# Joining the two products of a weight tile's high part in the output projections of a 1,024-wide model kernel

## The reference

```python
return u @ w2 + b2                    # Conformer convolution
return o.reshape(...) @ w_o           # differential attention
return (y * g) @ w_o                  # RWKV-7 time mix
return (u * s) @ w_out                # spatial gating
...
x = x + g_m * rms_norm(y, norm_g[l, 1])     # first block
x = x + _rmsnorm(h, norm_gains[i, 1])       # second block
```

## Time and profile before

| | |
|---|---|
| median of 3 runs | 1,419.88 us (1,414.57 to 1,428.73) |
| profiled execution, span from the first to the last instruction | 1,420.2 us |
| busy: PE / DVE / ACT / POOL | 97% / 74% / 52% / 15% |
| granted TensorE clock, mean | 0.996 of full speed |
| Square of unit 0 to Square of unit 7: conv_down | 124.45 to 144.41 us |
| the same: att_out | 467.24 to 486.54 us |
| the same: rw_out | 907.82 to 926.13 us |
| the same: sgu_out | 1,203.07 to 1,220.00 us |

### The profile page before, as it was taken

How to read it: one execution, slowest core, us unless ns; L and a number is a source line. 1 busy time by engine, 2 the same in 40 slices (tenths; PEclk the granted TensorE clock), 3 DMA queues, 4 the chain that set the end, 5 groups by cost and what they waited for, 6 DMA issues and landing times.

```text
span 1420.2 us, 30753 instructions
## 1 busy us (share of the span) xinstructions
PE 1375.6 (97%) x11830; PEld 1310.7 (92%) x11830; DVE 1049.1 (74%) x1649; ACT 733.2 (52%) x1194; POOL 219.2 (15%) x232
## 2 busy tenths in 40 slices
PE   8999999999999999999999999999999999999997
PEld 6998899999988899999878888799999998999997
DVE  7988799987887889974787965777774556677743
ACT  4547555644556556664366442554444447544442
POOL 0000133310000223320000010113320000133300
PEclk9999999999999999999999999999999999999999
DMA  9874367797663547675322300346666433466661
GB/s 377 303 258 171 123 226 234 258 394 252 205 226 105 208 165 254 216 232 173 151 98 90 120 2 2 116 133 186 188 208 203 141 115 120 144 197 197 208 205 69
DMA packets 68434, 258.20 MB, mean 182 GB/s; under 512 B 7545, under 2 KB 9857, under 8 KB 67970
## 3 DMA queue, kind: packets, MB, share of 16 engines
q1 hardware_dynamic: 68354, 257.10, 54.2%
HBM read 256.01 MB, written 1.06 MB: 181 GB/s over the span
## 4 chain that ended last, share of the span: by engine, by line
PE 81%; DVE 11%; ACT 3%; issue 2%; DMA 2%; DVEq 0%; ACTq 0%
PE ps L740 21%; PE ps L742 20%; PE ps L741 20%; PE ps L757 3%; DVE lo L1919 2%; PE ps L701 2%; PE ps L703 1%; PE ps L702 1%; ACT hi L1370 1%; DMA modraw<-in_wmod 1%; DVE U L2508 1%; DMA modlast<-in_wmod 1%; DVE products L2506 1%; DVE modraw L1925 1%; PE ps L764 1%
## 5 line engine op out<-in xcount | busy, mean ns | idle before, releaser
L1919 DVE TENSOR_TENSOR lo<-raw,hi 128x1024 fp32r<-128x1024 f32 (+1 forms) x350 | 476.5, 1378 | 168.5 <-ACT hi L1370 167.8
L740 PE MATMUL ps<-OH,lo 128*128 128x256 f32 x1920 | 540.8, 282 | 6.2 <-DVE lo L1919 6.0
L742 PE MATMUL ps<-OH,hi 128*128 128x256 f32 x1920 | 534.8, 279 | 0.0
L741 PE MATMUL ps<-OL,hi 128*128 128x256 f32 x1920 | 534.8, 279 | 0.0
L1370 ACT ACTIVATE hi<-raw 128x1024 fp32r<-128x1024 f32 (+1 forms) x350 | 381.0, 1112 | 10.4 <-DMA raw<-in_w 6.1
L740 PEld LDWEIGHTS ps<-OH,lo 128*128 128x128 f32 x1920 | 362.0, 189 | 12.7 <-DVE lo L1919 9.9
L741 PEld LDWEIGHTS ps<-OL,hi 128*128 128x128 f32 x1920 | 362.4, 189 | 0.0
L742 PEld LDWEIGHTS ps<-OH,hi 128*128 128x128 f32 x1920 | 361.0, 188 | 0.0
L740 PE MATMUL ps<-GH,lo 128*128 128x256 f32 x704 | 196.3, 279 | 0.0
L742 PE MATMUL ps<-GH,hi 128*128 128x256 f32 x704 | 196.2, 279 | 0.0
L741 PE MATMUL ps<-GL,hi 128*128 128x256 f32 x704 | 196.2, 279 | 0.0
(11 more groups left out here) (389 smaller groups left out, 2059.5 us busy)
## 6 DMA issues: line engine op xcount, KB each, us to landing
raw<-in_w SPq DMA_DIRECT2D x288, 512.0 KB, 3.9
raw<-in_w SPq DMA_DIRECT2D x64, 704.0 KB, 5.3
modraw<-in_wmod SPq DMA_DIRECT2D x71, 512.0 KB, 5.2
modlate<-in_wmod SPq DMA_DIRECT2D x10, 512.0 KB, 4.0
modlast<-in_wmod SPq DMA_DIRECT2D x7, 512.0 KB, 4.5
modfirst_a<-in_wmod SPq DMA_DIRECT2D x4, 512.0 KB, 11.4
modfirst_b<-in_wmod SPq DMA_DIRECT2D x4, 512.0 KB, 12.1
l<-in_lora_in SPq DMA_DIRECT2D x1, 1536.0 KB, 6.2
```

Source lines behind the costliest of these rows:

```text
L740: pe.matmul(bank[:, 0:T], lo[:, r, w], oh[:, k0 + k], start=first, stop=False)
L741: pe.matmul(bank[:, 0:T], hi[:, r, w], ol[:, k0 + k], start=False, stop=False)
L742: ins = pe.matmul(bank[:, 0:T], hi[:, r, w], oh[:, k0 + k], start=False, stop=final)
L1919: dve.tensor_tensor(lo[:, s, 0:kt * P], raw[:, s, 0:kt * P], hi[:, s, 0:kt * P].bitcast(F32), ALU.subtract).then_inc(lo_made, 1)
```

## The change

In the four projections the products hi x OL and hi x OH become one product of 512 columns: `OH` and `OL` now are the halves of one tile `OB`, and the product writes a whole PSUM bank, the OH columns in its first half, the OL columns in its second. lo x OH goes on adding into the first half. So a chunk takes two products instead of three (256 chunks in all four projections). Then VectorE adds the two halves of the bank into one of two slots of `xt` (`add_halves`, one instruction a unit, 32 in all), and ScalarE squares and scales from `xt` and no longer from PSUM. `add_halves` stands in VectorE's step u behind the low part of the tile of u + 2, and ahead of the riding sums. It waits for the unit's products and for the evacuation of unit u - 2. ScalarE's evacuation waits for it. Two waits on `tt_made` become waits on a second count of `tm_made`; the order there is the same. All other layers keep their three products.

```diff
-        OH = at(2, "OH", [P, DC, T], F32R)
-        OL = at(2, "OL", [P, DC, T], F32R, plus=OPERAND)
+        OB = at(2, "OB", [P, 2, DC, T], F32R)
+        OH, OL = OB[:, 0], OB[:, 1]
...
+            def split_products(bank, r, w, oh, ol, k, first, final, wide):
+
+                if wide and first:
+                    pe.matmul(bank[:, :], hi[:, r, w], OB[:, :, k], start=True, stop=False)
+                    return pe.matmul(bank[:, 0:T], lo[:, r, w], oh[:, k], start=False, stop=final)
+                pe.matmul(bank[:, 0:T], lo[:, r, w], oh[:, k], start=first, stop=False)
+                if wide:
+                    return pe.matmul(bank[:, :], hi[:, r, w], OB[:, :, k], start=False, stop=final)
+                pe.matmul(bank[:, 0:T], hi[:, r, w], ol[:, k], start=False, stop=False)
+                return pe.matmul(bank[:, 0:T], hi[:, r, w], oh[:, k], start=False, stop=final)
...
                     c = 2 * i + r // 2 if down else 4 * i + r
-                    src = PS[r - 1 if down else r][:, 0:T]
+                    if not down:
+                        act.wait_ge(S("halves_added"), c + (DC * (n // 2) + 1))
+                    src = PS[r - 1][:, 0:T] if down else xt[:, 2 + r % 2]
...
+            def add_halves(i, r, u):
+
+                dve.wait_ge(mm_done, u + 1)
+                wait(dve, evac_done, u - 1)
+                dve.tensor_reduce(xt[:, 2 + r % 2], PS[r][:, :].rearrange("p (h t) -> p t h", h=2), AX_X, ALU.add
+                                  ).then_inc(S("halves_added"), 1)
+
             def rows_out(i, r, u):
+
+                add_halves(i, r, u)
...
-            layer("att_out", peel_all=True, made=1)
+            layer("att_out", add_halves, peel_all=True, made=1)
...
-            layer("rw_out", third=True)
+            layer("rw_out", add_halves, third=True)
...
-            layer("sgu_out", third=True, made=1)
+            layer("sgu_out", add_halves, third=True, made=1)
```

More of the change, by code:

```diff
@@ L686, in filter_waves, with two_units @@
                 pe.wait_ge(S("dft_hi"), DC + 1)
-            def two_units(name, oh, ol, fresh, after_chunk, beside):
+            def split_products(bank, r, w, oh, ol, k, first, final, wide):
[7 more added lines that the diff above has]
+                return pe.matmul(bank[:, 0:T], hi[:, r, w], oh[:, k], start=False, stop=final)
+            def two_units(name, oh, ol, fresh, after_chunk, beside, wide):
                 start = START[name]
@@ L700, in two_units @@
                     for r in range(2):
-                        pe.matmul(PS[r][:, 0:T], lo[:, r, w], oh[:, k], start=(k == 0), stop=False)
-                        pe.matmul(PS[r][:, 0:T], hi[:, r, w], ol[:, k], start=False, stop=False)
-                        ins = pe.matmul(PS[r][:, 0:T], hi[:, r, w], oh[:, k], start=False, stop=(k == KT - 1))
+                        ins = split_products(PS[r], r, w, oh, ol, k, k == 0, k == KT - 1, wide)
                         if k == KT - 1:
@@ L711, in layer @@
             def layer(name, oh, ol, between=None, peel_first=False, fresh=False, after_chunk=None, beside=0, amid=None,
-                      peel_all=False, together=False):
+                      peel_all=False, together=False, wide=False):
                 kt, start = TILES[name], START[name]
@@ L720, in body @@
                     if both:
-                        two_units(name, oh, ol, fresh, after_chunk, beside)
+                        two_units(name, oh, ol, fresh, after_chunk, beside, wide)
                         for r in range(2):
@@ L739, in body @@
                             final = k == kt - 1 and (not down or r % 2 == 1)
-                            pe.matmul(bank[:, 0:T], lo[:, r, w], oh[:, k0 + k], start=first, stop=False)
-                            pe.matmul(bank[:, 0:T], hi[:, r, w], ol[:, k0 + k], start=False, stop=False)
-                            ins = pe.matmul(bank[:, 0:T], hi[:, r, w], oh[:, k0 + k], start=False, stop=final)
+                            ins = split_products(bank, r, w, oh, ol, k0 + k, first, final, wide)
                             if amid and k == kt // 2 - 1:
@@ L804, in out_layer @@
                 if n == 0:
-                    layer(name, oh, ol, square_sums, peel_all=True, together=True)
+                    layer(name, oh, ol, square_sums, peel_all=True, together=True, wide=True)
                     pe.wait_ge(S("ysq_ready"), DC - 1)
@@ L808, in out_layer @@
                 else:
-                    layer(name, oh, ol, between, together=(TILES[name] == KT), after_chunk=after_chunk)
+                    layer(name, oh, ol, between, together=(TILES[name] == KT), after_chunk=after_chunk, wide=(TILES[name] == KT))
                     pe.wait_ge(S("sq_added"), (DC - 2) * n)
@@ L1157, in first_t @@
             def first_t(tb):
-                pe.wait_ge(S("tt_made"), 1)
+                pe.wait_ge(S("tm_made"), 2)
                 pe.wait_ge(S("level_by_act"), tb + 2)
@@ L1796, in _ @@
                                ).then_inc(S("level_by_act"), 1)
-            act.wait_ge(S("tt_made"), 1)
+            act.wait_ge(S("tm_made"), 2)
             for tb in range(2):
@@ L2578, in _ @@
                           ).then_inc(S("tm_made"), 1)
-            dve.transpose(TTd[:].rearrange("p m t -> p t m"), U[:]).then_inc(S("tt_made"), 1)
+            dve.transpose(TTd[:].rearrange("p m t -> p t m"), U[:]).then_inc(S("tm_made"), 1)
             def level_copy(to, bank, rows, width):
@@ L2600, in _ @@
             third_block(1)
-            dve.wait_ge(S("tt_made"), 1)
+            dve.wait_ge(S("tm_made"), 2)
             dve.tensor_copy(TT[2 * BLK:3 * BLK, :, 2 * BLK:3 * BLK], TTd[2 * BLK:3 * BLK]).then_inc(S("level_by_dve"), 1)
```

## The result

| | before | after |
|---|---|---|
| median | 1,423.7 us (4 runs beside the change, 1,414.6 to 1,428.7) | 1,469.9 us (4 runs, 1,460.7 to 1,472.8) |
| ratio | | 1.031, 95% interval 1.025 to 1.036 |
| profiled execution: span; its own time | 1,420.2 us | 1,465.5 us; 1,467.3 us |

The change costs 46 us by the medians and 44 by the ratio.

What follows compares the result with a forecast made beforehand. TensorE bounds sgu_out and nearly rw_out before; after, a ScalarE-VectorE loop of 3.69 us a turn sets all four projections' pace. 1420.2 + 35.5 + 3.0 = 1458.7 us of span; forecast 1458 us, range 1443 to 1474.

Steps and rivals of the forecast that it cites:

- The turn: Loop from Square to Square through addition, copy, high part and low part: 3.69 us, 3.87 in conv_down, against TensorE's 2.72.
- The addition: VectorE's reduction of 512 elements read from PSUM, once a unit: 0.69 us, bounds 0.41 and 1.24.
- the rival of a double price: Addition reads alternating bank halves at double cost, 1.24 us, each turn 0.55 us longer: 1476 us, chance 0.09.
- Step 7 of rw_out and sgu_out: A second low part stands ahead of the last addition there: 1.14 us.
- The two riding sums in conv_down: Where two follow the addition, in units 0 and 4, VectorE needs 0.16 us more than the way by ScalarE.
- The first Square of rw_out: Unit 2's low part runs ahead of the first addition, so unit 0's Square comes 1.63 us later.
- By projection: Added time to unit 7's Square: sgu_out +10.8, rw_out +10.3, conv_down +8.2, att_out +7.3 us before 0.99 comes back.
- The clock behind the last unit: TensorE idles behind each projection's last unit, then runs at half clock: +0.75 us each, +3.0 in all, bounds 0 and 1.7 each.
- the 0.99 of the reciprocal: In att_out the reciprocal's low part now stands ahead of the last addition, giving back 0.99 us: +6.3 us.
- The products: A TensorE product of 512 columns takes 0.220 us, bounds 0.213 and 0.226; 1.5 us saved if TensorE remains the bound.
- The other side: TensorE remains the bound, only each projection's last addition shows: 1422 us, no change; chance 0.05.
- The forecast's own bounds: Cheap addition, PSUM prices and no clock loss give 1444 us; all four clock losses at 1.7 us give 1463.

Runs made afterwards that it cites:

- sum_first: Against the changed kernel, VectorE adds the halves of unit u before making the low part of unit u + 2's tile, in all four projections: 1,433.5 us, ratio 1.007.
- sum_twice: Against the changed kernel, every addition of the halves is made twice, the second behind the first: 1,499.1 us, ratio 1.053 to the kernel before.
- held_clock: Against the changed kernel, idle TensorE products fill the two pauses behind the last unit of each projection: 1,460.9 us, ratio 1.028 to the kernel before.
- no_sum: Against the changed kernel, 512-column products stay, VectorE adds nothing, ScalarE reads the bank's first half at once: 1,424.9 us, ratio 1.000 to the kernel before.
- sum_unread: Against the changed kernel, additions wait for their unit's evacuation and ScalarE reads the bank's first half without waiting for them: 1,438.7 us, ratio 1.010.

## Why the prediction was right, and where its sizes were off

- **The turn.** Right: 3.72 us in three projections for 3.69, 3.91 in conv_down for 3.87. From the rows: addition 0.68 and 0.10 to the Square, copy 0.33 later, high part 0.40 later, 1.04 long, 0.04 to the low part, 1.14 until the next addition. Only the way from VectorE to ScalarE was longer, 0.10 for 0.03: the prediction had taken it from the other direction. sum_first and sum_twice show that this sum is the pace, and not only that it fits.
- **The addition.** 0.683 us for 0.69; the rival of a double price has fallen.
- **The extras.** Step 7 of rw_out and sgu_out: 4.85 - 3.72 = 1.13 for 1.14. The two riding sums in conv_down: 4.00 and 4.02 against 3.91, 0.1 for 0.16. The first Square of rw_out: 1.69 later for 1.63. One was missed: a turn of 4.01 in rw_out, where a Square started 0.39 us behind its addition; no row says why.
- **By projection**, up to unit 7's Square: 8.4, 7.6, 10.8 and 11.2 us for 8.2, 7.3, 10.3 and 10.8. That 38.0 for 36.6 is mostly 28 turns times 0.03.
- **The clock behind the last unit.** Right in kind, too small: 1.0 us each, as held_clock shows, for 0.75. There are two pauses, and the half clock lasts 6.8 us, not the 3.4 of the row it was sized by. Against the first profile of before, att_out's tail became no longer (13.83 and 13.87 us), so that the 0.99 of the reciprocal came back as predicted. The second profile of before had a tail of 13.20 us, so most of that gain belongs to the one profile that the prediction was read from.
- **What bounds att_out.** The prediction put its 19.30 us down to the riding sums alone. The late transfers shown above had a part in them: the second profile has 17.98 us, and by that the sum for att_out, 0.74 + 25.83 - 17.98, would have been 8.6 us instead of 7.3.
- **The products.** I took 0.220 us for 512 columns; they take 0.226 to 0.235, mostly 0.235: twice a short one at either rate, the upper bound or a little above. It changed nothing, since TensorE is not the bound. The Trainium skill's page "TensorE: Matmul & The Clock Gate", section "Back-to-back issue gap", has 131 ns for them; the rows disagree, and no_sum shows no gain in time either.
- **The other side**, TensorE as the bound at 1,422 us, describes sum_first and no_sum, not the change: it needs the other order on VectorE.

The stages come to 41.2 us for 38.5. The rest of the way from 1,458 to 1,470 is not in the change's mechanism as I saw it: 4.2 us of the profile in untouched layers, 1.8 us between span and time of the profiled run, and 2.6 from that run to the median. The span was a low start: in all 32 runs of before beside the experiments it lies 2.1 to 2.2 us under the time, and the median of before beside the change was 1,423.7.

That the total lies inside the range was in part luck. The forecast's own bounds end at 1,463 us, and the range reached 1,474 only for the sake of the doubled addition, which did not happen. What was right is the mechanism, and that stands on the turns and on the order of VectorE, not on the total.

## What to carry to other kernels

Before an engine's result is put in the path of another, follow both written orders round: if the way back passes through work for a later unit, a loop has been made, and its sum, not any engine's load, is the new pace. Where 32 additions stand in VectorE's order was worth 31 us here, more than the 22 us that they take. And read single stages rather than totals: here two executions of one kernel differ by 7 us in one gated layer, and by 2 in one of the four stages.

## What the runs showed of the hardware

- The same products at the same granted clock run at one of two steady spacings for a whole layer, 113 or 117 ns (100 us / 885 or 852), and the cause is open.
- A pause of 2.6 us followed by one of 3.4 us came with 6.8 us of half clock; idle products in the pauses prevented it.
- VectorE's riding sum takes 1.22 us in conv_down and 1.75 in att_out of sum_first, where GpSimd adds two SBUF tiles at the time:

```profile
487.42 1.13 POOL L2747 TENSOR_TENSOR SQ<-SQ 128x256 f32<-128x256 f32 x1 [2.29 <-ACT SQ L1435]
```

  In sgu_out of the kernel before, where VectorE stood idle, the same addition took less:

```profile
1217.74 0.74 POOL L2729 TENSOR_TENSOR SQ<-SQ 128x256 f32<-128x256 f32 x1 [1.98 <-ACT SQ L1426]
```

  VectorE's is longer by 0.53 us and GpSimd's by 0.39 where they meet; no run here took one of them away. The Trainium skill's page "SBUF — State Buffer", section "Who interferes with whom", says that a VectorE instruction with two SBUF inputs contends with a GpSimd instruction that reads SBUF, and that `tensor_reduce` never does: this agrees. In sum_unread 16 of the 32 additions ran at the same time as one of GpSimd's, and they took 0.68 to 0.69 us as the others did; in this pair GpSimd's has its 0.74 too:

```profile
933.94 0.69 DVE L2201 TENSOR_REDUCE xt<-ps 128x256 f32<-128x512 f32 x1 [0.64 <-ACT Y L1439]
933.62 0.74 POOL L2753 TENSOR_TENSOR SQ<-SQ 128x256 f32<-128x256 f32 x1 [2.08 <-ACT SQ L1438]
```
